# Fewer semaphore reports in a gather-fed decoder trunk, and a key block that is loaded once

## The reference

```python
def peer_ffn(xn, w_query, subkeys, u_tbl, v_tbl):        # per chunk of 128 tokens
    q = (xc @ w_query).reshape(C, PEER_HEADS, 2, PEER_KEY_DIM)
    s = jnp.einsum('chpd,hpnd->chpn', q, subkeys)
    s1, i1 = lax.top_k(s[:, :, 0], PEER_TOPK)             # 16 of 128
    s2, i2 = lax.top_k(s[:, :, 1], PEER_TOPK)
    cand = (s1[..., :, None] + s2[..., None, :]).reshape(C, PEER_HEADS, 256)
    top_s, top_c = lax.top_k(cand, PEER_TOPK)             # 16 of 256
    idx = i1[top_c // 16] * 128 + i2[top_c % 16]
    gate = jax.nn.softmax(top_s, axis=-1)
    act = jax.nn.gelu(jnp.einsum('chkd,cd->chk', u_tbl[idx], xc), approximate=False)
    return jnp.einsum('chk,chkd->cd', gate * act, v_tbl[idx])
```

## Time and profile before

| | us |
|---|---|
| median of 3 runs | 1704.74 |
| lowest and highest of them | 1693.55, 1705.69 |
| the profiled execution, its device time | 1688.29 |
| the profiled execution, first to last instruction (span) | 1686.3 |

### The profile page before, as it was taken

How to read it: one execution, slowest core, us unless ns; L and a number is a source line. 1 busy time by engine, 2 the same in 40 slices (tenths; PEclk the granted TensorE clock), 3 DMA queues, 4 the chain that set the end, 5 groups by cost and what they waited for, 6 DMA issues and landing times.

```text
span 1686.3 us, 15100 instructions
## 1 busy us (share of the span) xinstructions
PE 1325.6 (79%) x4882; PEld 765.0 (45%) x4882; DVE 1052.9 (62%) x2495; ACT 366.5 (22%) x843; POOL 988.3 (59%) x1038
## 2 busy tenths in 40 slices
PE   9989788778768798849876899878987786665556
PEld 8976544344335454324543455535454442222222
DVE  3447477656766576655767845566667663866665
ACT  1111232112212223222212232133222221211101
POOL 0046466667666566646566765466666656666754
PEclk9989899889789898868898999889997988777778
DMA  9589999999999999999999999799999989899997
GB/s 333 178 302 339 359 340 358 375 391 382 381 368 355 342 401 406 399 408 404 385 404 378 360 400 404 293 397 328 373 406 365 349 299 385 323 365 368 377 334 301
DMA packets 197713, 607.66 MB, mean 360 GB/s; under 512 B 17597, under 2 KB 50437, under 8 KB 197637
## 3 DMA queue, kind: packets, MB, share of 16 engines
q0 software_dynamic: 147456, 536.94, 83.4%
q1 hardware_dynamic: 50048, 69.73, 11.9%
q10 hardware_dynamic: 132, 0.04, 0.0%
HBM read 605.59 MB, written 1.05 MB: 360 GB/s over the span
## 4 chain that ended last, share of the span: by engine, by line
PE 39%; DVE 16%; issue 14%; DMA 10%; POOL 10%; another core or an unknown queue 7%; ACT 3%; SPq 1%; POOLq 0%; DVEq 0%; ACTq 0%
PE sums L897 24%; POOL rows L654 10%; DVE rows L1707 8%; PE banks L754 8%; DMA rows<-in_peer_u,expert 6%; PE banks L771 4%; DMA rows<-in_peer_v,expert 3%; DVE h L1698 1%; DMA wring<-in_attn_w_q 1%; PE banks L780 1%; PE sums L763 1%; DMA h<-in_x 1%; DVE find L1606 1%; ACT soft_diag L1274 1%
## 5 line engine op out<-in xcount | busy, mean ns | idle before, releaser
L897 PE MATMUL sums<-rows,soft_diag 128*128 128x512 f32 x1764 | 865.4, 648 | 255.5 <-ACT soft_diag L1274 127.4
L654 POOL DMA_INDIRECT rows<-in_peer_v,expert x512 | 502.4, 981 | 448.8 <-PE sums L897 190.1
L1707 DVE SCALAR_TENSOR_TENSOR rows<-rows,xn_near 128x1024 f32<-128x1024 f32 x512 | 603.3, 1217 | 206.6 <-DMA rows<-in_peer_u,expert 176.6
L897 PEld LDWEIGHTS sums<-rows,soft_diag 128*128 128x128 f32 x1764 | 361.8, 209 | 727.7 <-issue 587.7
L654 POOL DMA_INDIRECT rows<-in_peer_u,expert x512 | 483.8, 945 | 235.8 <-issue 147.8
L1274 ACT ACTIVATE soft_diag<-ident,coef 128x128 f32<-128x128 f32 x446 | 138.4, 389 | 39.7 <-issue 22.6
L1266 ACT ACTIVATE gelu<-dots 128x8 f32<-128x8 f32 (+1 forms) x65 | 13.5, 208 | 582.7 <-DVE rows L1707 341.1
L1698 DVE SCALAR_TENSOR_TENSOR h<-rows,coef,h 128x1024 f32<-128x1024 f32 x63 | 80.7, 1281 | 0.0
L754 PE MATMUL banks<-xT,wring 128*128 128x128 f32 x512 | 65.0, 285 | 13.0 <-issue 10.6
L754 PEld LDWEIGHTS banks<-xT,wring 128*128 128x128 f32 x512 | 63.0, 201 | 18.0 <-issue 17.8
L1769 DVE SCALAR_TENSOR_TENSOR soft_diag<-banks,soft_diag 128x512 f32<-128x512 f32 (+1 forms) x8 | 7.7, 958 | 98.0 <-ACT soft_diag L1299 66.5
(11 more groups left out here) (209 smaller groups left out, 1019.7 us busy)
## 6 DMA issues: line engine op xcount, KB each, us to landing
wring<-in_w_kv SPq DMA_DIRECT2D x14, 1024.0 KB
rows<-in_peer_u,expert POOLq DMA_INDIRECT x512
rows<-in_peer_v,expert POOLq DMA_INDIRECT x512
wkept<-in_peer_w_query SPq DMA_DIRECT2D x8, 1024.0 KB
rows<-in_conv_w_in SPq DMA_DIRECT2D x7, 1024.0 KB, 11.9
wring<-in_peer_w_query SPq DMA_DIRECT2D x7, 1024.0 KB
wring<-in_attn_w_q SPq DMA_DIRECT2D x7, 1024.0 KB
wkept<-in_conv_w_out SPq DMA_DIRECT2D x4, 1024.0 KB
```

The source lines that it names most:

```text
L654: nc.gpsimd.indirect_dma_start(row[j], None, table, bass.IndirectOffsetOnAxis(ap=expert[n % 2][:, k:k + 1], axis=0)).then_inc(landed[j], 16)
L897: last = nc.tensor.matmul(sums[:, half, :], diag[:, k % GROUP, :], v_row[k % V_SLOTS][:, half * 512:(half + 1) * 512], start=(first and k ...
L1707: nc.vector.scalar_tensor_tensor(out=u_row[j], in0=u_row[j], scalar=1.0, in1=xn_near[:, :, :].rearrange("p a d -> p (a d)"), op0=ALU.mult, ...
```

## The change

1. **Dots.** `dot_done` is incremented by dots 3 and 7 of a group only (`DOTS_BY = 4`); `u` gather j waits for the fourth or the eighth dot.
2. **Used rows.** `v_used` is incremented by rows 3 and 6 only. `v` gathers 0 to 3 wait for row 3, gathers 4 to 6 for row 6; ACT's diagonals wait in the same way.
3. **Diagonals.** `diag_ready` is incremented by diagonals 0 and 6 only. PE's row 0 waits for diagonal 0, rows 1 to 6 wait for diagonal 6.
4. **Search.** The copy of the scores goes; the two sides are searched side by side, so that one mark stands for two instructions; 13 marks are left of 25.
5. **Key block.** It is loaded once, in three transfers, into the second-chunk halves of `keyT` and `value`, which are not written before the second chunk, and read from there by PE in both chunks. Both `stream_key` blocks of 1 MB leave SP's list; `values(0, 0)`'s second half takes over the wait that `key(0, 0)` had.

```diff
+    DOTS_BY = GROUP // 2
+    USED_AFTER = (3, 6)
+    DIAG_AFTER = (0, 6)
+    def dots_count(K, j):
+        return GROUP // DOTS_BY * K + j // DOTS_BY + 1
+    def used_count(K, row):
+        return len(USED_AFTER) * K + sum(r < row for r in USED_AFTER) + 1
...
-    stream_key(0, 0)
     stream_qry(0, 1)
...
-    stream_key(1, 0)
...
+                if m == BLOCK["qry", 0, 0]:
+                    sp.wait_ge(bank_done, FILL["out0", 1] + 1)
+                    w_key = w_kv.rearrange("(k p) n -> p k n", p=P)
+                    sp.dma_start(value_half, w_key[:, 0:KT // 2, 0:COLS]).then_inc(key_landed, 16)
+                    for s in range(2):
+                        sp.dma_start(keyT_half[:, :, s, :], w_key[:, KT // 2:, s * P:(s + 1) * P]).then_inc(key_landed, 16)
...
-                    pool.wait_ge(dot_done, GROUP * (K - 1) + j + 1)
+                    pool.wait_ge(dot_done, dots_count(K - 1, j))
...
-                        pool.wait_ge(v_used, BY_PE * (K - 1) + j + 1)
+                        pool.wait_ge(v_used, used_count(K - 1, j))
...
-                    last.then_inc(v_used, 1)
+                    if k % GROUP in USED_AFTER:
+                        last.then_inc(v_used, 1)
...
-                s = mark(nc.vector.tensor_copy(srch, src))
-                for p in range(2):
-                    e = top16(side_v[:, p, :], side_i[:, p, :], srch[:, p * KEYS:(p + 1) * KEYS],
-                              srch2[:, p * KEYS:(p + 1) * KEYS], s)
+                for values, _, all_keys, _ in sides:
+                    best = nc.vector.max(values[:, 0:8], all_keys)
+                need(mark(best))
+                for values, _, all_keys, rest in sides:
+                    replaced = nc.vector.match_replace(rest, values[:, 0:8], all_keys, FOUND)
+                r = mark(replaced)
+                for values, indices, all_keys, _ in sides:
+                    nc.vector.max_index(indices[:, 0:8], values[:, 0:8], all_keys)
+                need(r)
...
-                                                   accum_out=dots[b][:, k:k + 1]).then_inc(dot_done, 1)
+                    if j % DOTS_BY == DOTS_BY - 1:
+                        dot.then_inc(dot_done, 1)
```

More of the change, by code:

```diff
@@ L66, in trunk, with diag_count @@
     BY_PE = GROUP - 1
-    PE_ROWS = GROUPS * BY_PE
+    DOTS_BY = GROUP // 2
+    USED_AFTER = (3, 6)
+    DIAG_AFTER = (0, 6)
     SLOTS = HEADS * GROUPS
+    def dots_count(K, j):
+        return GROUP // DOTS_BY * K + j // DOTS_BY + 1
+    def used_count(K, row):
+        return len(USED_AFTER) * K + sum(r < row for r in USED_AFTER) + 1
+    def diag_count(K, row):
+        return len(DIAG_AFTER) * K + sum(r < row for r in DIAG_AFTER) + 1
     fills, FILL = [], {}
@@ L300, in placed @@
             PLACE[BLOCK[(*name, kh) if len(slots) > 1 else name]] = slot
-    def stream_key(c, slot):
-        stream_whole(w_kv, 0, ("key", c, 0), "key", c, 0)
-        placed([slot], "key", c, 0)
     def stream_qry(c, slot):
@@ L731, in weights_of, with key_to_features @@
                 return w_place[w_slot[m]]
+            def key_to_features(c):
+                bank = take("key", c, 0)
+                pe.wait_ge(key_landed, 16 * 3)
+                for s in range(2):
+                    for k in range(KT):
+                        last = nc.tensor.matmul(bank[:, s * P:(s + 1) * P], kept_key(k, s), kvT[:, k, :],
+                                                start=(k == 0), stop=(k == KT - 1))
+                last.then_inc(bank_done, 1)
             def halves_to_features(m, part, second_half_of=None):
@@ L1002, in mixer_slot @@
                             score(0, *asked)
-                    to_features(take("key", c, 0), weights_of("key", c, 0), kvT, P)
+                    key_to_features(c)
                     to_features(take("qry", c, 0), weights_of("qry", c, 0), mixT, P)
@@ L1272, in weigh @@
                     if not (n == 0 and g == 0):
-                        act.wait_ge(v_used, PE_ROWS * n + BY_PE * (g - 1) + min(j, BY_PE - 1) + 1)
-                    nc.scalar.activation(diag[:, j, :], ident[:], ACT.Copy, scale=coef[b][:, k:k + 1]).then_inc(diag_ready, 1)
+                        act.wait_ge(v_used, used_count(GROUPS * n + g - 1, min(j, BY_PE - 1)))
+                    shaped = nc.scalar.activation(diag[:, j, :], ident[:], ACT.Copy, scale=coef[b][:, k:k + 1])
+                    if part is not None or j in DIAG_AFTER:
+                        shaped.then_inc(diag_ready, 1)
             def weigh_pair(i, last=False):
@@ L1675, in find_experts @@
-                need(d)
+                src = score_at(0, 1) if n == 1 else scores[:, at, :]
+                sides = [(side_v[:, p, :], side_i[:, p, :], src[:, p * KEYS:(p + 1) * KEYS], srch2[:, p * KEYS:(p + 1) * KEYS])
+                         for p in range(2)]
+                for values, _, all_keys, _ in sides:
[3 more added lines that the diff above has]
+                    replaced = nc.vector.match_replace(rest, values[:, 0:8], all_keys, FOUND)
@@ new lines, in find_experts @@
+                r = mark(replaced)
+                for values, indices, all_keys, _ in sides:
+                    nc.vector.max_index(indices[:, 0:8], values[:, 0:8], all_keys)
+                need(r)
+                for values, _, _, rest in sides:
+                    best = nc.vector.max(values[:, 8:16], rest)
+                need(mark(best))
+                for values, indices, _, rest in sides:
+                    nc.vector.max_index(indices[:, 8:16], values[:, 8:16], rest)
+                need(mark(nc.vector.tensor_tensor(cand.rearrange("p (a b) -> p a b", b=TOPK),
+                                                  side_v[:, 0, :].unsqueeze(2).to_broadcast([P, TOPK, TOPK]),
+                                                  side_v[:, 1, :].unsqueeze(1).to_broadcast([P, TOPK, TOPK]), ALU.add)))
@@ new lines, in find_experts @@
+                need(mark(nc.vector.max(top[b][:, 0:8], cand)))
+                r = mark(nc.vector.match_replace(cand2, top[b][:, 0:8], cand, FOUND))
+                nc.vector.tensor_scalar(negmax[:, b:b + 1], top[b][:, 0:1], -1.0, None, ALU.mult)
+                nc.vector.max_index(cand_i[:, 0:8], top[b][:, 0:8], cand)
+                need(r)
+                nc.vector.max(top[b][:, 8:16], cand2).then_inc(top_ready, 1)
+                dve.wait_ge(top_ready, n + 1)
+                need(mark(nc.vector.max_index(cand_i[:, 8:16], top[b][:, 8:16], cand2)))
@@ new lines, in find_experts @@
+                nc.vector.tensor_scalar(digit[:, 0, :], cand_i[:], 4, None, ALU.logical_shift_right)
+                need(mark(nc.vector.tensor_scalar(digit[:, 1, :], cand_i[:], TOPK - 1, None, ALU.bitwise_and)))
+                need(mark(nc.vector.tensor_tensor(pick.rearrange("p a k j -> p (a k) j"),
+                                                  digit[:].rearrange("p a k -> p (a k)").unsqueeze(2).to_broadcast([P, 2 * TOPK, TOPK]),
+                                                  iota[:].unsqueeze(1).to_broadcast([P, 2 * TOPK, TOPK]), ALU.is_equal)))
@@ new lines, in find_experts @@
+                need(mark(nc.vector.tensor_tensor(pick, pick, side_i[:].unsqueeze(2).to_broadcast([P, 2, TOPK, TOPK]), ALU.mult)))
+                need(mark(nc.vector.tensor_reduce(picked[:].rearrange("p a k -> p (a k)"),
+                                                  pick.rearrange("p a k j -> p (a k) j"), AX_X, ALU.add)))
+                need(mark(nc.vector.scalar_tensor_tensor(out=expert_f[:], in0=picked[:, 0, :], scalar=float(KEYS),
+                                                         in1=picked[:, 1, :], op0=ALU.mult, op1=ALU.add)))
@@ L1924, in _ @@
             for half, cols in enumerate(halves_of_d):
-                dve.wait_ge(v_used, PE_ROWS * last + BY_PE + len(TAIL_PE) + half)
+                dve.wait_ge(v_used, used_count(GROUPS * last, BY_PE - 1) + len(TAIL_PE) + half)
                 nc.vector.tensor_tensor(h[:, 1, cols], sums[:, half, :], h[:, 1, cols], ALU.add).then_inc(stream_ready, 1)
```

53 lines of the change are left out of this document (18 added, 35 removed).

## The result

The changed kernel takes **1750.61 us** (median of 4 runs, 1735.63 to 1760.76); the kernel before takes 1700.26 us beside it (4 runs, 1693.55 to 1705.69). The ratio is **1.0304, 95% interval 1.0256 to 1.0352**: slower by 50 us, where 1682 us and a gain of 1.3% were forecast. The profiled execution took 1746.63 us, with a span of 1744.7 us.

The account below looks back on a forecast made before the run. DMA traffic, nearly all gathers, was taken as the bound, with reports late at its ceiling. Terms -2.6 - 12 - 21 + 13 = -22.6 us gave 1665.7 profiled, 1682 us as timed with the 16.5 us offset; range 1632 to 1718.

Parts of the forecast that it names:

- Reports have a service time and queue up: Reports between engines: about 1 to 2 us each at the DMA ceiling, queued behind earlier ones, so fewer reports pay.
- the search term: DVE's disturbed searches: 98 us over costs about 25 us of DMA time; 13 of 25 marks saves half, -12 us.
- Key block -2.6 us: First key block's loads: 1.05 MB less traffic at 410 GB/s, -2.6 us; PE's waits for streamed weights taken as 0.
- The quiet search: DVE's undisturbed search falls from 9.0 to about 8.3 us; 22 us of DVE time in all, hidden.
- The sign I had named: DVE's search: the longest ones should fall below 17 us if the forecast holds.
- Used rows, -21 us of 35 pauses: POOL's pauses on reports in some 35 disturbed groups: 1.8 us each, 63 us if all go; a third taken, -21 us.
- rival C: Reports are late because DMA is full, whatever their number; pauses stay, time about 1704 us; chance 0.25.
- Used rows where POOL follows PE, +13 us, bounds 0 and +40: In 16 groups two more gathers follow PE's last row, 2.5 us each, 40 us unhidden; a third taken, +13 us.
- D: Coarser used rows decide, in followed and paused groups: slower, +67 us at worst, about +30, 1735 us; chance 0.15.
- The closing sentence: PE at the DMA ceiling: if it still crawls there, the forecast is wrong above all, and the delay isn't of reports.
- Dots and diagonals 0: POOL's waits for dots and PE's for diagonals, each told twice a group: 0 us each, as engines have slack.
- three dips of 0.31 MB: DMA windows in POOL's pauses: one dip fills one to three 3 us windows, 0.7 to 2.6 us of DMA time.

Follow-up runs that it names:

- e3: Kernel before with the first key block kept on chip and used rows told at rows 3 and 6 only: 1740.92 us, ratio 1.0297.
- e4: Kernel before, first key block kept on chip, used rows told after all seven rows but awaited coarsely by POOL and ACT: 1738.24 us, ratio 1.0305.
- e2: Changed kernel with used rows, dots and diagonals told and awaited one by one; new search and key block stay: 1685.86 us, ratio 0.9992.
- e6: Kernel before with the first key block kept on chip; ACT alone waits coarsely for used rows, POOL row by row: 1689.16 us, ratio 0.9977.
- e1: Changed kernel with only the used rows told and awaited one by one again: 1682.45 us, ratio 1.0006.
- e7: Kernel before, first key block kept on chip; POOL's v gathers 0 to 3 wait for row 3, 4 to 6 for their own: 1752.42 us, ratio 1.0247.
- e11: Kernel before with the first key block kept on chip and two POOL memsets, each waited for, ahead of each gather: 1680.37 us, ratio 0.9935.
- e9: Changed kernel with one 128 x 1 POOL memset, waited for, ahead of each gather: 1710.32 us, ratio 1.0108.
- e10: Kernel before with the first key block kept on chip and one POOL memset, waited for, ahead of each gather: 1682.13 us, ratio 0.9884.

## Why the prediction was wrong

Two steps failed: that reports are late by their number, which made 33 us of gain, and that the used rows cost POOL only its own time behind row 6, which put the cost at 13 us where it was 58.

**Reports have a service time and queue up** (the reading on which 33 us of the gain rested). Wrong. Seven reports or two make no difference (e3, e4), nor do 25 marks or 13 beyond 0.4% (e2), and the stalls of the searches don't follow the marks: against their time on the second kind of chip (279 us with the old search, 258 with the new) the 31 searches run over by 107 us in the kernel before, 117 in e3 and 92 in e6, all with 25 marks, and by 165 us in the changed kernel, 101 in e1 and 77 in e2, all with 13. The row I built on, 0.97 us with one mark out and 3.90 us with one queued between the earlier trace rows, was two examples of a wide scatter: 50.2 us in all ahead of L1709, which has one report out. That reports are late was right; that they are late by their number was the step that failed.

The rule of the page "VectorE: DVE Perf Modes" of the Trainium skill, section "The DRAIN you can't avoid", that "the semaphore costs nothing extra here", gave the search term 0. The time agrees with it (e2, 0.9992); the traces of the first kind of chip show besides that a wait for DVE's own mark can idle it up to 3.90 us.

**Key block -2.6 us.** Twelve blocks and 606.61 MB came as said. The gain is under what e2 can tell (0.4%).

**Search.** The quiet search was to fall from 9.0 to 8.3 us. On the undisturbed chip it goes from 333.72 to 342.71 us in the kernel before and from 335.15 to 343.54 us in the changed one, 9.0 to 8.4 us, and 8.2 us at the shortest. Hidden, as said. The disturbed searches were to give -12; they gave nothing that e2 can tell. The sign I had named, the longest search below 17 us, failed: 21.5 us in the changed kernel, 23.4 us in e2, 24.2 us before.

**Used rows, -21 us of 35 pauses.** The pauses stayed at 3.1 to 3.6 us and the beat at 23.2 us. Here rival C was right: the pauses stay, whatever the number of reports. (Its time, near 1704 us, was not.) Also right was that row 3 instead of row 0 is free there, as POOL goes on long after both are done.

**Used rows where POOL follows PE, +13 us, bounds 0 and +40.** The place was right in part and the size was the miss: 58 us. (Of the five groups, 2, 38 and 42 followed PE in the kernel before; 23 and 35 had a single pause of 2.2 us ahead of v gather 0.) I priced only the late end, two gathers or 2.5 us a group behind row 6, and gave the late start of gather 0, three rows or some 5 us later, no term at all; e7 shows that the head alone costs 2.5%. The chain of steps I didn't follow was: with row 3 instead of row 0 the empty queues stay empty longer, they are refilled in a burst, a burst reaches the ceiling, and PE crawls, as the earlier trace rows had shown, now in its projections, where the kernel before had 6 us of it in these groups and the changed one 37. That is 6 to 10 us in each of five groups, and less in some others. I had both halves, PE's crawl at the ceiling and the gathers that follow PE, and did not put the one behind the other.

**The rivals.** D, the coarser rows decide, gave 1735 us and chance 0.15; it had the direction, and the result is above it. It charged the paused groups for the wait for row 6; what two of them lost was lost ahead of gather 0. The closing sentence was the right one: if PE still crawls at the ceiling, the delay isn't of reports.

**Dots and diagonals 0.** Nothing against it (e1, 1.0006, but with an interval of 0.9% either way).

**Readings.** The earlier trace rows shows six slices under 9, not four, and three dips of 0.31 MB at 410 GB/s are 2.3 us, not 2.6. Neither moves the forecast.

## What to carry to other kernels

A wait that paces an engine which issues transfers may be worth more than the time it costs: before making it coarser, ask at what rate the transfers go out behind it, and whether that rate is above what the queues drain. Price a change of a wait by the idle time it makes and by what the burst after it does to the engines that are then at work, not by the issuer's own instructions. And where an engine's matmuls come singly at full traffic, try a short pause ahead of each transfer, and measure it on more than one chip: here two memsets gained 0.65% on one kind and lost 8% on the other.

## What the runs showed of the hardware

- The same kernel takes about 1690 us on some chips and 1555 us on others (8%; two chips of each kind, each measured at its own hour). On the first kind its runs spread from 1661 to 1702 us, on the second they stay within 4 us, but for one at 2297 us. On the first, PE's matmuls come singly or a few at a time with gaps of up to 3.1 us, and reports up to 16 us late, while gathers are asked for at 423 GB/s; on the second neither is seen at the same 400 to 410 GB/s.
- On the first kind the lateness is gone when a gather of 0.524 MB is asked for each 1.48 us (354 GB/s; e11), although the traffic, weights included, still holds 398 to 412 GB/s for 72 us. At 1.32 us (397 GB/s) some is left: 14.8 us ahead of the lookup in e9 and 19.2 in e10, where unpaced kernels have from 19.7 (e2) to 36.0 us (e4).
- A memset of 128 x 1 on POOL (0.11 us) and the wait for it add 0.08 us to the step between two gathers, since the idle time ahead of the gather is then 0.27 instead of 0.30 us; a second pair adds 0.16 us more.
